# Differential attention's value products turned, and the heads' norms taken through DRAM rows, with the steps three ticks sooner

## The reference, cut to what matters

```python
s = jnp.einsum('bihce,bjhce->bhcij', qblk, k) * (Dh ** -0.5)
p = jax.nn.softmax(s, axis=-1)
a = p[:, :, 0] - lam * p[:, :, 1]
yd = jnp.einsum('bhij,bjhe->bihe', a, v)             # 8 heads, 512 queries, 128 wide
yd = rms_norm(yd, diff_subln) * (1.0 - lambda_init)  # over the 128 of each query
yd = yd.reshape(B, S, DIFF_V_WIDTH) * jax.nn.silu(zd)
pb = yd @ w_proj_b
```

## Time and profile before

| what | us |
|---|---|
| median of 3 runs (lowest, highest) | 801.75 (800.88, 803.82) |
| the profiled execution: its own time | 801.21 |
| its span in the profile | 799.1 |
| TensorE busy, share of the span | 778.6, 97% |
| VectorE, ScalarE, GpSimd busy | 420.2, 359.9, 452.4 |
| mean granted clock of TensorE | 0.992 of full speed |

### The profile page before, as it was taken

How to read it: one execution, slowest core, us unless ns; L and a number is a source line. 1 busy time by engine, 2 the same in 40 slices (tenths; PEclk the granted TensorE clock), 3 DMA queues, 4 the chain that set the end, 5 groups by cost and what they waited for, 6 DMA issues and landing times.

```text
span 799.1 us, 12588 instructions
## 1 busy us (share of the span) xinstructions
PE 778.6 (97%) x4590; PEld 656.9 (82%) x4590; DVE 420.2 (53%) x692; ACT 359.9 (45%) x777; POOL 452.4 (57%) x577
## 2 busy tenths in 40 slices
PE   4999999999999999999999999999999999999997
PEld 3787898888888888898797888888787878878997
DVE  4766664635455443344675576487557445324432
ACT  5555535545444444343464555455556333314311
POOL 7854545446656654369663696596454287837200
PEclk9799999999999999999999999999999999999999
DMA  9955323233343432352431433242212145615431
GB/s 317 348 168 155 86 84 104 81 98 115 107 119 105 121 107 80 107 151 81 140 97 54 121 105 121 78 123 76 82 34 74 35 151 213 208 53 177 139 106 53
DMA packets 87075, 95.38 MB, mean 119 GB/s; under 512 B 9405, under 2 KB 78310, under 8 KB 87014
## 3 DMA queue, kind: packets, MB, share of 16 engines
q1 hardware_dynamic: 86944, 94.56, 38.3%
q10 hardware_dynamic: 70, 0.02, 0.0%
HBM read 78.53 MB, written 5.54 MB: 105 GB/s over the span
## 4 chain that ended last, share of the span: by engine, by line
PE 90%; issue 3%; POOL 3%; DVE 1%; DMA 1%; ACT 1%; SPq 0%; DVEq 0%; POOLq 0%; ACTq 0%
PE proj L1747 64%; PE sums L1670 4%; PE proj L1867 4%; PE score L1586 4%; PE turned L1638 3%; PE score L1620 3%; PE proj L1796 2%; PE sums L1672 2%; POOL w_lo L819 1%; PE score L1608 1%; DMA x_in<-in_x 1%; PE score L1796 1%; PE turned L1680 0%; PE turned L1694 0%; POOL merged L796 0%
## 5 line engine op out<-in xcount | busy, mean ns | idle before, releaser
L819 POOL TENSOR_TENSOR w_lo<-raw,w_hi 128x256 fp32r<-128x256 f32 x376 | 299.9, 829 | 212.7 <-ACT w_hi L932 212.7
L1747 PE MATMUL proj<-h_hi,w_hi 128*128 128x512 f32 x560 | 229.4, 410 | 0.1
L1747 PE MATMUL proj<-h_hi,w_lo 128*128 128x512 f32 x560 | 219.3, 392 | 0.0
L1747 PE MATMUL proj<-h_lo,w_hi 128*128 128x512 f32 x560 | 218.7, 391 | 0.0
L1747 PEld LDWEIGHTS proj<-h_hi,w_hi 128*128 128x128 f32 x560 | 105.2, 188 | 30.4 <-issue 9.6
L1747 PEld LDWEIGHTS proj<-h_hi,w_lo 128*128 128x128 f32 x560 | 105.1, 188 | 23.2
L1747 PEld LDWEIGHTS proj<-h_lo,w_hi 128*128 128x128 f32 x560 | 105.5, 188 | 19.1 <-issue 0.5
L932 ACT ACTIVATE w_hi<-raw 128x1024 fp32r<-128x1024 f32 x96 | 100.4, 1054 | 15.7 <-PE proj L1747 11.2
L1380 DVE TENSOR_TENSOR at_lo<-turned,at_hi 128x512 fp32r<-128x512 f32 x64 | 44.1, 689 | 80.6 <-ACT at_hi L1070 80.0
L848 POOL TENSOR_TENSOR rope_x<-rope_x,cos_t 128x512 f32<-128x512 f32 x36 | 53.4, 1484 | 51.6 <-DMA rope_s<-rope_x 51.6
L1670 PE MATMUL sums<-v,at_hi 128*128 128x128 f32 (+1 forms) x256 | 60.8, 307 | 0.0
(11 more groups left out here) (291 smaller groups left out, 1479.7 us busy)
## 6 DMA issues: line engine op xcount, KB each, us to landing
raw<-in_w_in SPq DMA_DIRECT2D x85, 512.0 KB, 3.6
rope_s<-rope_x SPq DMA_DIRECT2D x144, 64.0 KB, 2.0
ada<-in_w_ada SPq DMA_DIRECT2D x24, 256.0 KB, 7.1
raw<-in_w_proj_b SPq DMA_DIRECT2D x8, 512.0 KB, 3.4
zd<-in_w_ada SPq DMA_DIRECT2D x8, 512.0 KB, 4.6
raw<-in_w_out SPq DMA_DIRECT2D x8, 512.0 KB, 4.2
rows_in<-window_rows SPq DMA_DIRECT2D x4, 792.0 KB, 5.8
window_rows<-rows_out SPq DMA_DIRECT2D x4, 528.0 KB, 5.0
```

Of the source, the lines that this page charges most:

```text
L819: nc.gpsimd.tensor_tensor(lo[:, k, :], raw_place(n)[:, k, :], hi.bitcast(F32)[:, k, :], ALU.subtract).then_inc(w_lo_done, 1)
L1747: ins = mm(dst, left, right, start=k == 0 and n == 0, stop=k == nk - 1 and n == 2, skip_group_check=tile.b == 2)
```

## The change

- **Value products.** Two steps of a differential head (parts 0 and 1, or 2 and 3) are multiplied together in the second one's tick. v is the weights now, and the turned probabilities of both steps are streamed, 256 columns, so `sums` holds the head turned: its 128 channels on the partitions, 512 queries in the bank. `at_hi` and `at_lo` get three slots instead of two, as the first step of a pair waits for the second.
- **Norms.** `copy_sums`, `peak`, `scale_head` and `head_turn` are gone for these heads. VectorE multiplies `sums` by the gate at once (`head_gate`); ScalarE squares `sums` and cuts the squares; TensorE sums them over the channels with two matmuls whose weights are one column of 1/128 (`head_share`), which gives one row of 512 numbers. ScalarE copies the row and stores it to DRAM (`norm_rows`), reads it back as 128 x 4 (`norm_cols`, 512 pieces of 4 bytes); GpSimd makes the eight small operations; ScalarE stores the result as 128 runs of 16 bytes (`norm_store`) and loads it on all partitions (`norm_load`, 128 x 2 KB). VectorE multiplies the head by it, reading with a stride of four (`head_norm`).
- **Ticks.** The steps of stages 6 to 9 begin at `t0[n + 1] - 3`. For a head whose last products are at tick pv: share at pv + 2, columns pv + 3, GpSimd pv + 4, store pv + 5, load pv + 6, `head_norm` pv + 7, which is the tick at which `gate_head` stood before. The last head's pv is tick 157, its share 159.
- The squares use the first half of `gate_row`, the row the second half; the copies of the windowed v blocks get a place of their own (`vt_copy`).

```diff
-        self.copies = self.group or head % 2
+        self.copies = self.group in (1, 2) or (self.group == 0 and head % 2)
...
-        begin = t0[n + 1] + (0 if n else 2) + (g in (1, 2))
+        begin = t0[n + 1] - 3 if g == 3 else t0[n + 1] + (0 if n else 2) + (g in (1, 2))
...
+    at_slot, at_before, user = {}, {}, {}
+    for s in steps:
+        n = (0, 2, 1, 2)[s.part] if s.group == 3 else s.s % 2
+        at_slot[s.s], at_before[s.s] = n, user.get(n)
+        user[n] = s.s + (s.group == 3 and s.part % 2 == 0)
     diff_ends = [s for s in head_ends if s.group == 3]
-    scale_at = by_tick(diff_ends, lambda s: s.pv + 3)
+    head_lo_at = by_tick(diff_ends, lambda s: s.pv + 1)
...
-    y_at = by_tick(diff_ends, lambda s: free_turn(s.pv + 4))
+    y_at = by_tick(diff_ends, lambda s: free_turn(s.pv + 2))
+    cols_at = by_tick(diff_ends, lambda s: s.pv + 3)
+    norm_at = by_tick(diff_ends, lambda s: s.pv + 4)
+    store_at = by_tick(diff_ends, lambda s: s.pv + 5)
+    load_at = by_tick(diff_ends, lambda s: s.pv + 6)
+    final_at = by_tick(diff_ends, lambda s: s.pv + 7)
...
+        square = gate_row[:, 0:S]
+
+        def at_place(s):
+
+            n = at_slot[s.s]
+            return at_hi[:, n, :], at_lo[:, n, :]
+
+        def at_free(engine, s):
+
+            if at_before[s.s] is not None:
+                engine.wait_ge(pv_done, at_before[s.s] + 1)
...
+                for s in norm_at(t):
+                    n = diff_ends.index(s)
+                    y = lambda i: ystat[:, i, :]
+                    den = dens[:, s.hd % 2, 0, :]
+                    pts, ptt = nc.gpsimd.tensor_scalar, nc.gpsimd.tensor_tensor
+                    pool.wait_ge(row_landed, 16 * (n + 1))
+                    link(ptt(y(0), den, den, ALU.mult))
+                    link(pts(y(1), y(0), lam[:, 7:8], None, ALU.mult))
+                    link(ptt(y(1), y(1), y(3), ALU.add))
+                    link(ptt(y(1), y(1), half_c[:, 0:4], ALU.pow))
+                    link(pts(y(0), y(0), st[:, 60:61], None, ALU.mult))
+                    link(ptt(y(0), y(3), y(0), ALU.subtract))
+                    link(pts(y(0), y(0), 0.0, 2.0 ** -32, ALU.is_lt, ALU.mult))
+                    ptt(y(1), y(1), y(0), ALU.mult).then_inc(pow_done, 1)
...
             def head_squares(s):
                 n = diff_ends.index(s)
-                act.wait_ge(peak_done, n + 1)
-                for qt in range(NT):
-                    ins = nc.scalar.activation(junk[:], head_sums[:, s.hd % 2, qt * P:(qt + 1) * P], ACT.Square,
-                                               scale=ystat[:, 2, qt:qt + 1], accum_out=ystat[:, 3, qt:qt + 1])
-                    ins.then_inc(squares_done, 1)
-                    act.wait_ge(squares_done, NT * n + qt + 1)
+                act.wait_ge(head_read, n + 1)
+                act.wait_ge(head_done, n)
+                nc.scalar.activation(square, sums[:], ACT.Square, scale=st[:, 58:59]).then_inc(squares_done, 1)
+                act.wait_ge(squares_done, 2 * n + 1)
+                nc.scalar.activation(square_hi[:], square, ACT.Copy).then_inc(squares_done, 1)
+
+            def norm_rows(s):
+                n = diff_ends.index(s)
+                act.wait_ge(t_filled, turned_no["y", s.hd] + 1)
+                if n:
+                    act.wait_ge(pow_done, n)
+                nc.scalar.activation(gate_row[0:1, S:2 * S], turned[0:1, :], ACT.Copy).then_inc(t_read, 1)
+                act.wait_ge(t_read, turned_no["y", s.hd] + 1)
+                act.dma_start(share_rows[n:n + 1, :], gate_row[0:1, S:2 * S]).then_inc(row_stored, 16)
+
+            def norm_cols(s):
+                n = diff_ends.index(s)
+                act.wait_ge(row_stored, 16 * (n + 1))
+                act.dma_start(ystat[:, 3, :], share_rows[n].rearrange("(c p) -> p c", p=P), allow_slow_non_contiguous=True).then_inc(row_landed, 16)
+
+            def norm_store(s):
+                n = diff_ends.index(s)
+                act.wait_ge(pow_done, n + 1)
+                act.dma_start(rstd_rows[n].rearrange("(p c) -> p c", p=P), ystat[:, 1, :]).then_inc(rstd_stored, 16)
+
+            def norm_load(s):
+                n = diff_ends.index(s)
+                act.wait_ge(rstd_stored, 16 * (n + 1))
+                act.dma_start(square, rstd_rows[n].partition_broadcast(P)).then_inc(rstd_landed, 16)
...
+                for s in y_at(t):
+                    norm_rows(s)
+                for s in cols_at(t):
+                    norm_cols(s)
+                for s in store_at(t):
+                    norm_store(s)
+                for s in load_at(t):
+                    norm_load(s)
...
-                if s.group == 3:
-                    n = diff_ends.index(next(e for e in diff_ends if e.hd == s.hd))
-                    if n >= 2:
-                        dve.wait_ge(t_filled, turned_no["y", s.hd - 2] + 1)
-                    at = 2 * P * (s.part % 2)
-                    nc.vector.tensor_reduce(head_sums[:, s.hd % 2, s.part * P:(s.part + 1) * P],
-                                            sums[:, at:at + 2 * P].rearrange("p (w e) -> p e w", w=2),
-                                            AX_X, ALU.add).then_inc(sums_copied, 1)
-                elif s.group == 0:
+                if s.group == 0:
...
-            def peak(s):
+            def head_gate(s):
                 n = diff_ends.index(s)
-                dve.wait_ge(sums_copied, COPIED_BEFORE[s.s] + 1)
-                link(nc.vector.reciprocal(ystat[:, 0, :], dens[:, s.hd % 2, 0, :]))
-                nc.vector.tensor_reduce(ystat[:, 2, :], ystat[:, 0:2, :].rearrange("p a q -> p q a"), AX_X,
-                                        ALU.mult).then_inc(peak_done, 1)
-
-            def scale_head(s):
+                dve.wait_ge(pv_done, s.s + 1)
+                dve.wait_ge(z_done, Z_DONE[n])
+                stt(out=zd[:, n, :], in0=sums[:], scalar=cols[:, 41:42], in1=zd[:, n, :],
+                    op0=ALU.mult, op1=ALU.mult).then_inc(head_read, 1)
+
+            def head_lo(s):
                 n = diff_ends.index(s)
-                dve.wait_ge(pow_done, n + 1)
-                for qt in range(NT):
-                    rows_ = head_sums[:, s.hd % 2, qt * P:(qt + 1) * P]
-                    ts_(rows_, rows_, ystat[:, 5, qt:qt + 1], None, ALU.mult).then_inc(y_scaled, 1)
-
-            def gate_head(s):
+                dve.wait_ge(squares_done, 2 * n + 2)
+                tt_(square_lo[:], square, square_hi[:].bitcast(F32), ALU.subtract).then_inc(square_lo_done, 1)
+
+            def head_norm(s):
                 n = diff_ends.index(s)
-                dve.wait_ge(t_filled, turned_no["y", s.hd] + 1)
-                dve.wait_ge(z_done, Z_DONE[n])
-                stt(out=zd[:, n, :], in0=turned[:], scalar=cols[:, 41:42], in1=zd[:, n, :],
-                    op0=ALU.mult, op1=ALU.mult).then_inc(t_read, 1)
+                dve.wait_ge(rstd_landed, 16 * (n + 1))
+                dve.wait_ge(head_read, n + 1)
+                head = zd[:, n, :].rearrange("p (c q) -> p c q", c=NT)
+                tt_(head, head, square.rearrange("p (q c) -> p c q", c=NT), ALU.mult).then_inc(head_done, 1)
...
+                if s.group == 3 and s.part % 2 == 0:
+                    return
...
+                if s.group == 3:
+                    pair = s.part // 2
+                    if pair == 0:
+                        n = diff_ends.index(next(e for e in diff_ends if e.hd == s.hd))
+                        pe.wait_ge(sums_copied, COPIED_BEFORE[s.s])
+                        pe.wait_ge(squares_done, 2 * n)
+                        pe.wait_ge(head_read, n)
+                    to = sums[:, 2 * P * pair:2 * P * (pair + 1)]
+                    for kt in range(NT):
+                        keys_ = slice(kt * P, (kt + 1) * P)
+                        v_hi, v_lo = (v[:, kt, w, s.head * P:(s.head + 1) * P] for w in range(2))
+                        hi, lo = (at[:, pair:3:2 - pair, keys_] for at in (at_hi, at_lo))
+                        mm(to, v_hi, hi, start=kt == 0, stop=False, skip_group_check=True)
+                        mm(to, v_hi, lo, start=False, stop=False, skip_group_check=True)
+                        ins = mm(to, v_lo, hi, start=False, stop=kt == NT - 1, skip_group_check=True)
+                    ins.then_inc(pv_done, 2)
+                    return
...
-            def head_turn(s):
+            def head_share(s):
+                n = diff_ends.index(s)
                 turn_bank(("y", s.hd))
-                pe.wait_ge(y_scaled, NT * (diff_ends.index(s) + 1))
-                for qt in range(NT):
-                    ins = nc.tensor.transpose(turned[:, qt * P:(qt + 1) * P], head_sums[:, s.hd % 2, qt * P:(qt + 1) * P], ident[:])
-                ins.then_inc(t_filled, 1)
+                if n == 0:
+                    pe.wait_ge(share_done, 1)
+                pe.wait_ge(square_lo_done, n + 1)
+                mm(turned[0:1, :], share[:, 0:1], square_hi[:], start=True, stop=False)
```

(43 more changed lines are left out.)

72 lines of the change are left out of this document (34 added, 38 removed).

## The result

The changed kernel takes 804.52 us in the median (802.07 to 807.48, 15 runs) against 801.01 for the kernel before on the same chip (15 runs): ratio 1.0044, 95% interval 1.0034 to 1.0055. The forecast was 801.0. The time lies in the range (796.8 to 806.5), but it is a small loss where a small gain was forecast. The profiled execution took 805.44 (span 803.6), 0.9 over its median; the one of before 801.2 (span 799.1).

The account below looks back on a forecast made before the run. TensorE's issued work was taken to bound the kernel, others mattering only where it waits. Terms -4.8 + 0.2 + 0.4 + 1.35 + 2.0 = -0.85 on 801.2, plus 0.5, gave 800.9; forecast 801.0 us, range 796.8 to 806.5.

Parts of the forecast that it names:

- Part 1: Value products of the differential stages: 12 matmuls of 256 columns per pair of steps, 0.30 us gained each, -4.8 us.
- Rival (c): Value products: spacing of the new matmuls is not 0.12 us, first term becomes +4.8, total 810.6 us; chance 0.05.
- the +0.2 for the first product of a head: TensorE's first product of each head waits for four semaphores instead of two: +0.2 us for eight heads, between 0 and 0.8.
- Part 2: Head's turn on TensorE: two 512-column matmuls replace four transposes, +0.09 us a head, taken as +0.4 in all.
- Part 3: VectorE, ScalarE, GpSimd: their changed work stays off the path while probabilities are ready for their transposes; worth 0.
- The slack of 2.05 us: In a steady step, the join ends at 573.74 and TensorE's transposes come at 575.79, leaving 2.05 us.
- Part 4: Steps three ticks sooner: stage 6's first scores wait 1.65 us for k's low part, 0.3 comes back; +1.35 us.
- Part 5: Last head's norm round trip, 18.0 us against 15.4 available: TensorE waits 3.0 us against 1.0 before, +2.0 us.
- (b): Broadcast load arrives too late in every head, delaying VectorE and TensorE's transposes: +9.6, 810.5 us; chance 0.15.
- (a): Round trip is quick, transfers near 2.0 us, so the products' gain stands nearly alone: 797.9 us; chance 0.2.
- The sign for seeing it: Waits expected on k_lo (about 1.6 us) and yd_late_lo (about 3 us), no other TensorE wait above 0.3 us.
- the tail: Last head's norm round trip at the end of the kernel: TensorE's wait grows from 1.0 to 3.0 us, +2.0.

Follow-up runs that it names:

- the three moves: Changed kernel with GpSimd's norm ahead of its tick's cuts, window rows' loads two ticks later, head 6's low part ahead of the last head's norm: 798.06 us.

## Why the prediction was wrong

- **Part 1, products: right.** -4.8 forecast; the pair is 1.44 against 1.74, and the run without the trip fits it in time. Rival (c) is out. The term left out that a projection started late behind the old products, about 1.0 us in all, so the saving was somewhat larger; the +0.2 for the first product of a head was not measured by itself.
- **Part 2, the head's turn: slightly too dear.** 0.47 against 0.37 with 0.09 of slow start behind it: about 0, not +0.4.
- **Part 3, "Worth 0": this is the step that failed.** The slack of 2.05 us was read rightly, but only work was weighed against it, not a wait in program order. The change put `norm_store` into ScalarE's list ahead of the rotary cut, and its wait is for GpSimd, whose norm stands behind two cuts of 3.3 and 3.7 us. I had the pieces: I wrote that GpSimd's operations wait for a DMA while cuts queue behind them. It was the other way round, and I did not ask who stands in line behind the store. By the trace it cost 3.7 us in three heads, and moving the norm ahead of the cuts gave back 3.2. VectorE's crowding, on the same slack, cost 1.4 more by the trace; no run separates it.
- **Part 4, the first place: right.** +1.35 forecast, +1.27 measured (1.53 against 0.26), with the cause named, as the run with later loads shows.
- **Part 5, the last head: right in size, for partly wrong terms.** +2.0 forecast, +1.6 measured. The broadcast load landed in 4.0 (4.0 forecast), the store in 2.6 (2.0), the column read in 2.1 (3.3), but GpSimd's cut took back most of that difference: column landed 639.6, norm begun 640.60. That the errors cancelled is luck. What failed beside it is the assumption that a stall costs its own length: the matmuls behind it ran at the lower clock for 1.6 us.
- **The Trainium skill on the load.** By the Trainium skill, "DMA: Bandwidth & Descriptors", anatomy of one DMA, the estimate for 256 KB is 2.6 us; the eight loads have a median of 3.7 in this trace (3.1 to 4.2), so the rows were the better guide. That section is on transfers issued by GpSimd, and these are ScalarE's. The rule of the Trainium skill's same page against a strided last dimension ("Rules for kernel authors") did not decide here: 512 pieces of 4 bytes landed in 2.1 us in the median (2.1 to 2.5).
- **The rivals.** (b) had the right kind, a wait that pushes joins past the slack, but at the wrong instruction: the load never reached 5.6 us; the store ahead of it was the one that held ScalarE. (a) had the column read right and missed what took up the time that it saved.
- **The sign for seeing it** was right: "at no other place a TensorE wait above 0.3 us". Five were.

Together: -0.85 forecast, + 5.2 for the transposes, + 1.6 for the clock, - 0.4 for the tail, - 0.1 for the first place, - 2.2 for TensorE's own work (-6.4 against -4.2) and + 1.4 for the delay of this execution in the opening is +4.6, the growth of the span. That the time still lay in the stated range is luck: the 5.2 us in no term were partly covered by a saving that was in no term either.

## What to carry to other kernels

When a DMA of a long chain is issued by an engine that also computes, write down for its wait both who releases it, in that engine's own program order, and what stands behind it; a wait in the middle of its list spends the slack of all that follows (1.53 us of it cost nothing here, 4.08 cost 1.45). Each shortened link shows the next, and gains measured alone need not add up; three cheap reorderings made of a change that lost 0.4% one that gains 0.4%. When a stall of the bottleneck engine can't be removed, ready work can be moved in front of it: here that took the stall and the low clock out of the profile, while the medians don't yet tell the gain from that of the three moves.

## What the runs showed of the hardware

The clock behind a stall. In the fourteen profiles, from 330 us on, TensorE stood still for 1.8 us or more twelve times, and behind ten of them the matmuls of 512 columns followed at 0.43 instead of 0.23 for some six to eleven starts (1.6 us in the changed kernel), then at 0.23 again; of 53 stalls between 0.3 and 1.77 us none had that behind it. The two exceptions stood for 2.04 and 1.81. The stall near 70 us is in all fourteen: with the low clock behind it in four (2.20, 2.40, 2.74 and 3.78 us), without it at 2.10 and 2.54 and in the eight from 1.33 to 1.68. The last stall filled, or emptied by moved work, left the clock at 1.00 in the profiles of the three runs that did it, against two of the nine profiles in which it stood for 1.8 us or more; that the stall is the cause is likely by this, and not shown by the times. What decides between the cases with and without it stays open.

An elementwise operation of VectorE that runs beside GpSimd's cuts varies: the last `head_norm` took 1.28 us in the changed kernel and 2.99 with GpSimd's norm first. The order on GpSimd is not what decides: it took 2.94 in the run with nine more matmuls, where VectorE's and GpSimd's programs are those of the changed kernel, and 1.4 in the three versions with three moves, which have GpSimd's norm first. That this comes from the two engines' running together was not tested.
